# The input panels of block 1 by head halves, with most of them and of the first output panel beside the attention units

## The chip, the cores and the metric

The kernel runs on one core of a Trainium2 chip. Its time is the device time of one launch in microseconds (us), and lower is better. TensorE (PE) does the matrix products, VectorE (DVE), ScalarE (ACT) and GpSimd (POOL) the rest, and SyncE (SP) issues the DMAs.

## What is computed

Two transformer blocks in fp32 on 512 tokens of width 1024. Block 1 is where the change lies:

```python
h = rms_norm(x, norm1_g[l])
proj = h @ w_in[l]                       # 1024 -> q, k, v (512 each: 8 heads of 64) and u (512)
q = rms_norm(q, q_norm_g[l]); k = rms_norm(k, k_norm_g[l])
a = neighbourhood_attention(q, k, v, rpb[l])   # 8 rows x 64 columns, 16 columns wide, with a bias table
p = multiscale_pool(u, w_pool[l], pool_scale[l])
x = x + jnp.concatenate([a, p], axis=-1) @ w_out[l]
x = x + (silu(h2 @ w_gate[l]) * (h2 @ w_up[l])) @ w_down[l]    # h2 = rms_norm(x, norm2_g[l]), 2816 wide
```

Block 2 has a sliding-window attention, a convolution branch, gates and a second feed-forward part, and ends in a norm.

## The kernel before

Activations stand transposed on chip: a chunk is 128 channels by 512 tokens. All weights pass in **panels** of 256 columns, in two blocks of 128 (m = 0, 1), through two slots. For each block SP loads 512 KB into `w_stage`, ACT rounds it to `w_hi` (`high_part`, L539), POOL subtracts the rest into `w_lo` (`low_part`, L462), and PE makes three products of 128x128 by 128x512 for each of 8 chunks k (`step`, L1163): high by high, high by low, low by high. So a panel is 48 products. `open_block` (L1175) waits for the low part and for the bank's last result to have been taken. The order of each engine's work is written out by hand, with semaphores between them.

Block 1 starts so. PE turns x (L1205 to 1212), DVE copies it to `xT` (L814) and makes `h_lo` (L795), ACT makes `h_hi` (L572). Input panels 0 to 7 hold q (0, 1), k (2, 3), v (4, 5) and u (6, 7), and are taken in this order. The norm of x is applied behind the products: ACT squares 8 chunks (L578), DVE adds them (L790, `add_squares`), PE sums over partitions (`norm_sum`, L1197), ACT takes the root (`norm_root`), DVE the reciprocal `rs` (`norm_factor`, L803). Each q and k chunk c is then squared (ACT), summed by head (PE, `qk_sum`, L1214), rooted (ACT, `qk_roots`, L590) and scaled by a reciprocal (DVE, `qk_norm`, L839). v is turned (`turn_v`) and copied (`v_copy`).

Attention has 16 **units**, each two blocks of 128 queries of one head, and goes in pairs on PE (loop at L1328): `score_pair` (L1281, 8 products), `value_pair` of four units back (L1293, 16 products), `turn_probs` of two units back (L1273). DVE reads the scores (L880), ACT makes the exponentials (`exps`, L611), DVE divides (`normalise`, L863). Units 0 to 7 use heads 0 to 3, units 8 to 15 heads 4 to 7. The table `BESIDE1` (L296) lays pieces of panels 6 and 7 between the units' products, one piece being one block and two chunks k, 6 products. `POOL_AT`, `SUMS_AT` and `MEANS_AT` set at which unit the work of the pooling branch is done. Behind the units comes the first output panel (`OUT1`, L1362 to 1372).

```python
        steps1 = [s for steps in beside(IN1 + 6, 2, 1) for s in steps]
        for count in (4, 1, 1, 2, 1, 1, 0, 2, 1, 0, 0, 3, 0, 0, 0, 0, 0, 0, 0):
```

SP loads x and panels 0 and 1, then the small vectors (L410 to 417), panels 2 and 3, 32 short-run DMAs of the attention bias (L425 to 429), and then the rest in order.

## Time and profile before

| what | value |
|---|---|
| median of 3 runs | 1248.16 us (1247.87 to 1249.33) |
| the profiled execution | 1247.56 us |
| its span on the core | 1245.8 us |
| PE busy | 1214.3 us (97%) |
| DVE, POOL, ACT busy | 629.5, 553.1, 486.7 us |
| DMA | 115 MB, mean 92 GB/s |

The span runs from the first to the last instruction that the profiler saw, and the execution's own time is 1.76 us longer. The page gives shares of the whole span. What a stage costs is read from stretches of time and from the timeline of one engine, where the words in brackets behind an instruction are the idle time ahead of it and what ended it.

### The profile page before, as it was taken

The numbers are of one execution on the slowest core, as the hardware profiler recorded it, in microseconds if no ns is written. First come the engines' busy times: TensorE is split into PE (matmuls) and PEld (weight loads), VectorE is DVE, ScalarE is ACT, GpSimd is POOL, SyncE is SP. The second block draws the span as 40 slices with busy tenths as digits, with TensorE's granted clock in tenths as the row PEclk, the third lists the DMA queues.
The fourth block names the chain that finished last, engine by engine and source line by source line (L and its number), as shares of the span: only waits on it lengthen the run. The fifth ranks groups of instructions, "written<-read, shape, count | busy, mean of one in ns | idle before, by whom it ended". The sixth has DMA issues, their size and how long they took to land.

```text
span 1245.8 us, 16589 instructions
## 1 busy us (share of the span) xinstructions
PE 1214.3 (97%) x5568; PEld 986.4 (79%) x5568; DVE 629.5 (51%) x854; ACT 486.7 (39%) x715; POOL 553.1 (44%) x311
## 2 busy tenths in 40 slices
PE   7899899999999999999999999999999999999997
PEld 5677678888888888888877887788888888888876
DVE  6589855432134413466387422266677136622654
ACT  5234634533222222244465432344455234322344
POOL 4393123444444344455423545654355444443441
PEclk9899999999999999999999999999999999999999
DMA  6732113332433333234320223434233333333211
GB/s 189 148 90 87 35 36 100 101 88 80 119 97 90 100 102 93 72 89 118 102 68 27 78 82 101 118 102 118 77 92 105 100 100 88 98 102 102 84 51 68
DMA packets 219505, 115.14 MB, mean 92 GB/s; under 512 B 4195, under 2 KB 217921, under 8 KB 219457
## 3 DMA queue, kind: packets, MB, share of 16 engines
q1 hardware_dynamic: 219441, 114.50, 31.9%
q8 instruction: 30, 0.49, 0.2%
q14 instruction: 18, 0.15, 0.0%
q10 hardware_dynamic: 16, 0.00, 0.0%
HBM read 112.39 MB, written 2.10 MB: 92 GB/s over the span
## 4 chain that ended last, share of the span: by engine, by line
issue 43%; PE 28%; POOL 20%; DVE 4%; ACT 2%; DMA 1%; POOLq 1%; SPq 0%; DVEq 0%; ACTq 0%
PE ps L1170 27%; POOL w_lo L466 19%; DVE sq_sum L790 1%; ACT w_hi L546 1%; DVE mid L1016 1%; DMA w_stage<-in_w_in 1%; DVE mid L783 1%; POOL mid L459 1%; DVE mid L1026 1%; ACT mid L681 0%; DVE h_lo L795 0%; ACT g_hi L686 0%; SPq L373 0%; ACT mid L678 0%; DVE rs L805 0%
## 5 line engine op out<-in xcount | busy, mean ns | idle before, releaser
L466 POOL TENSOR_TENSOR w_lo<-w_stage,w_hi 128x1024 fp32r<-128x1024 f32 x218 | 535.0, 2464 | 666.3 <-ACT w_hi L546 666.2
L1170 PE MATMUL ps<-h_hi,w_hi 128*128 128x512 f32 x1104 | 438.5, 397 | 1.8 <-POOL w_lo L466 1.1
L1170 PE MATMUL ps<-h_hi,w_lo 128*128 128x512 f32 x1104 | 431.3, 391 | 0.0
L1170 PE MATMUL ps<-h_lo,w_hi 128*128 128x512 f32 x1104 | 430.9, 390 | 0.0
L546 ACT ACTIVATE w_hi<-w_stage 128x1024 fp32r<-128x1024 f32 x218 | 227.0, 1056 | 367.9 <-PE ps L1170 364.1
L1170 PEld LDWEIGHTS ps<-h_hi,w_hi 128*128 128x128 f32 x1104 | 208.1, 188 | 51.2 <-issue 7.3
L1170 PEld LDWEIGHTS ps<-h_lo,w_hi 128*128 128x128 f32 x1104 | 208.2, 189 | 44.4 <-issue 2.2
L1170 PEld LDWEIGHTS ps<-h_hi,w_lo 128*128 128x128 f32 x1104 | 207.9, 188 | 44.0
L1170 PE MATMUL ps<-g_hi,w_hi 128*128 128x512 f32 x544 | 212.0, 390 | 2.0 <-DVE g_lo L1028 1.9
L1170 PE MATMUL ps<-g_lo,w_hi 128*128 128x512 f32 x544 | 211.7, 389 | 0.0
L1170 PE MATMUL ps<-g_hi,w_lo 128*128 128x512 f32 x544 | 211.6, 389 | 0.0
L783 DVE TENSOR_TENSOR mid<-ps,rs 128x512 f32<-128x512 f32 x130 | 88.1, 687 | 233.6 <-PE ps L1170 233.5
L979 DVE TENSOR_TENSOR xT<-xT,ps 128x512 f32 x64 | 43.4, 686 | 165.4 <-PE ps L1170 165.3
L1170 PEld LDWEIGHTS ps<-g_hi,w_hi 128*128 128x128 f32 x544 | 102.1, 188 | 24.2 <-DVE g_lo L1028 2.8
L1170 PEld LDWEIGHTS ps<-g_hi,w_lo 128*128 128x128 f32 x544 | 102.1, 188 | 21.3
L1170 PEld LDWEIGHTS ps<-g_lo,w_hi 128*128 128x128 f32 x544 | 102.1, 188 | 21.1
L1016 DVE SCALAR_TENSOR_TENSOR mid<-mid,vec 128x512 f32<-128x512 f32 x88 | 101.7, 1213 | 25.2 <-ACT mid L678 25.2
L1026 DVE TENSOR_TENSOR mid<-mid 128x512 f32<-128x512 f32 x44 | 62.3, 1416 | 27.8 <-ACT mid L684 25.1
L686 ACT ACTIVATE g_hi<-mid 128x512 f32 x44 | 27.8, 632 | 74.7 <-DVE mid L1026 74.7
L684 ACT ACTIVATE mid<-mid 128x512 f32<-128x512 f32 x44 | 27.5, 625 | 72.3 <-DVE mid L1016 72.3
L790 DVE TENSOR_TENSOR sq_sum<-sq_sum,sq 128x512 f32<-128x512 f32 x32 | 47.1, 1473 | 13.7 <-ACT sq L658 13.7
L1028 DVE TENSOR_TENSOR g_lo<-mid,g_hi 128x512 f32 x44 | 31.6, 718 | 43.9 <-ACT g_hi L686 43.9
(141 smaller groups left out, 686.2 us busy)
## 6 DMA issues: line engine op xcount, KB each, us to landing
w_stage<-in_w_up SPq DMA_DIRECT2D x66, 512.0 KB, 3.8
w_stage<-in_w_in SPq DMA_DIRECT2D x50, 512.0 KB, 3.9
w_stage<-in_w_down SPq DMA_DIRECT2D x32, 512.0 KB, 3.6
...
```

What stands on the lines that cost most here:

```text
L459: return pool.affine_select(out=ap, in_=in_, compare_op=cmp, fill=fill, base=base, pattern=pattern, channel_multiplier=mult)
L466: pool.tensor_tensor(w_lo[:, s, c], w_stage[:, s, c], low_of(w_hi[:, s, c]), ALU.subtract).then_inc(w_lo_ready, 1)
L546: act.activation(w_hi[:, s, c], w_stage[:, s, c], ACT.Copy).then_inc(w_hi_ready, 1)
L684: act.activation(gate, gate, ACT.Silu).then_inc(f_silu, 1)
L686: act.activation(chunk(g_hi, 2 * i + j), up, ACT.Copy).then_inc(f_hi, 1)
L783: dve.tensor_tensor(out, bank(par, m), rs[:, :], ALU.mult).then_inc(evacuated, 1)
L790: dve.tensor_tensor(sq_sum[:, :], sq_sum[:, :], squares, ALU.add).then_inc(sq_added, 1)
L979: dve.tensor_tensor(chunk(xT, m), chunk(xT, m), bank(par, e), ALU.add).then_inc(evacuated, 1)
L1016: dve.scalar_tensor_tensor(o, f_in[:, 2 * e + j, 1 - tap:1 - tap + T], col(f"fconv{1 - tap}", c + FC * e), o, ALU.mult, ALU.add)\
L1026: dve.tensor_tensor(up, gate, up, ALU.mult).then_inc(f_prod, 1)
L1028: dve.tensor_tensor(chunk(g_lo, 2 * i + j), up, low_of(chunk(g_hi, 2 * i + j)), ALU.subtract).then_inc(f_ready, 1)
L1170: ins = pe.matmul(bank(par if banks is None else banks, m), a, b, start=first and i == 0, stop=last and i == 2)
```

## The change

The order of the input panels becomes 0, 2, 4, 1, 3, 5, 6, 7: q, k and v of heads 0 to 3 first. The first four panels of the new order and three pieces of the fifth (`AHEAD1`) are done ahead of the units, and the 29 pieces that are left lie beside units 0 to 11. The second half of q, k and v is normed, taken and turned between units, with the roots at units 1 and 4. Of the first output panel, 6 of its 8 chunks lie beside units 12 to 17, and 2 behind the units. At the start, panel 0 is loaded and split in halves of 4 chunks k, its first products stand ahead of the second half of the turns of x, `h_lo` is made from the PSUM bank and not from `xT`, and the squares of x come from the untransposed x with the sum of each token in one accumulator (4 of 128x1024), which DVE spreads on a diagonal for PE's sum. The bias rows come in 16 DMAs, not 32, and ahead of the small vectors. What is computed is the same.

```diff
-        steps1 = [s for steps in beside(IN1 + 6, 2, 1) for s in steps]
...
+        IN1_ORDER = (0, 2, 4, 1, 3, 5, 6, 7)
+
+        QK = [("q", 0), ("q", 1), ("k", 0), ("k", 1), ("q", 2), ("q", 3), ("k", 2), ("k", 3)]
+        QK_PANEL = (0, 0, 1, 1, 3, 3, 4, 4)
+        HALF_QK = len(QK) // 2
...
+        def qk_bank(c):
+            return 5 + c % 2 if c < HALF_QK else 2 * (QK_PANEL[c] % 2) + c % 2
+
+        steps1 = [s for steps in beside(IN1 + 4, 4, 1) for s in steps]
+        AHEAD1, steps1 = steps1[:3], steps1[3:]
...
+        for count in (3, 3, 3, 3, 3, 2, 2, 2, 2, 2, 2, 2, 0, 0, 0, 0, 0, 0, 0):
             BESIDE1.append(steps1[:count])
             steps1 = steps1[count:]
-
-        SUMS_AT = {0: (0, (0,)), 4: (1, (0,)), 5: (1, (1,)), 8: (2, (0,)), 9: (2, (1,)), 10: (2, (2,)),
+        assert not steps1
+
+        def v_bank(a):
+            return ps[:, 6 + a, :] if a < 2 else bank(5, a - 2)
+
+
+        QK_SUMS_AT = {0: (4, 5), 3: (6, 7)}
+        QK_ROOTS_AT = {1: (4, 5), 4: (6, 7)}
+        QK_NORM_AT = {1: 4, 2: 5, 4: 6, 5: 7}
+        K_TAKE_AT, K_SQUARES_AT, V_TAKE_AT, V_TURN_AT = 2, 3, 5, 6
+        SUMS_AT = {7: (0, (0,)), 8: (1, (0, 1)), 10: (2, (0,)), 11: (2, (1, 2)),
                    12: (3, (0,)), 13: (3, (1,)), 14: (3, (2,)), 15: (3, (3,))}
...
+            def load_first(k0, signals):
+
+                for m in range(2):
+                    sp.dma_start(
...
             load_x(0)
-            for n in range(2):
-                load(IN1 + n, n % 2, [cols(w_in[0], n * 256), cols(w_in[0], n * 256 + P)])
...
+            load_first(0, first_landed)
+            load_x(1)
+            load_first(KC // 2, w_landed[0])
+            load(IN1 + 1, 1, [cols(w_in[0], IN1_ORDER[1] * 256), cols(w_in[0], IN1_ORDER[1] * 256 + P)])
...
+            sp.wait_ge(bias_cleared, 1)
+            for c, j, count in BIAS_ROWS:
...
             for tile, r, src in vec_loads[1:]:
                 sp.dma_start(vec_rows[r:r + src.shape[0], tile, :], src).then_inc(vec_landed, 16)
...
-            for n in range(2, 4):
-                load(IN1 + n, n % 2, [cols(w_in[0], n * 256), cols(w_in[0], n * 256 + P)])
...
-            sp.wait_ge(bias_cleared, 1)
...
-            for c in range(16):
-                for dst, shift, first in ((bias_in, c, 7), (bias_in_edge, 0, 15 - c)):
...
-            load_pairs(IN1 + 4, 4, w_in[0], 1024)
+            for n in range(2, 8):
+                load(IN1 + n, n % 2, [cols(w_in[0], IN1_ORDER[n] * 256), cols(w_in[0], IN1_ORDER[n] * 256 + P)])
+                if n == 3:
+                    sp.dma_start(w_pool_sb[:, :, :], w_pool[0].rearrange("g c d -> c g d")).then_inc(pool_w_landed, 16)
...
+            for half, (signal, done) in enumerate(((first_hi, first_lo), (w_hi_ready, w_lo_ready))):
+                for m in range(2):
+                    pool.wait_ge(signal, m + 1)
+                    c = slice(m * HALF + half * FIRST, m * HALF + (half + 1) * FIRST)
+                    pool.tensor_tensor(w_lo[:, 0, c], w_stage[:, 0, c], low_of(w_hi[:, 0, c]),
+                                       ALU.subtract).then_inc(done, 1)
...
+            low_part(1, 1)
+            low_part(2, 0)
+            pool.wait_ge(bias_landed, 16 * len(BIAS_ROWS))
+            pool.wait_ge(sq_added, NT)
+            for h in range(HEADS // 2):
+                bias_tables(h)
+            low_part(3, 1)
+            for h in range(HEADS // 2, HEADS):
+                bias_tables(h)
+            low_part(4, 0)
...
+            def first_high(half, m, signal, done):
+                act.wait_ge(signal[m], 16)
+                c = slice(m * HALF + half * FIRST, m * HALF + (half + 1) * FIRST)
+                act.activation(w_hi[:, 0, c], w_stage[:, 0, c], ACT.Copy).then_inc(done, 1)
...
                 if m < 2:
-                    high_part(0, 0, m)
+                    first_high(0, m, first_landed, first_hi)
+                if m in (4, 5):
+                    first_high(1, m - 4, w_landed[0], w_hi_ready)
             high_part(1, 1, 0)
             high_part(1, 1, 1)
-            for m in range(KC):
-                act.activation(chunk(sq_start, m), chunk(xT, m), ACT.Square).then_inc(x_squared, 1)
...
+            for t in range(NT):
+                for e in range(2):
+                    act.wait_ge(x_landed[e][t], 16)
+                act.activation(sq_start[:, t, :], x_in[:, t, :], ACT.Square,
+                               accum_out=x_sq[:, t:t + 1]).then_inc(x_squared, 1)
...
+                for c in QK_ROOTS_AT.get(u, ()):
+                    qk_roots(c)
+                if u == K_SQUARES_AT:
+                    for c in (6, 7):
+                        qk_squares(c)
...
-            for m in range(KC):
-                add_squares(0, m, chunk(sq_start, m))
+
+            def x_low_of_bank(m):
+                dve.wait_ge(x_scaled, m + 1)
+                dve.scalar_tensor_tensor(chunk(h_lo, m), ps[:, m % 4, :], col("norm1", m),
+                                         low_of(chunk(h_hi, m)), ALU.mult, ALU.subtract)\
+                   .then_inc(h_ready, 1)
...
+            for t in range(NT):
+                dve.wait_ge(x_squared, t + 1)
+                dve.tensor_scalar(sq_sum[:, t * P:(t + 1) * P], ident[:, :], x_sq[:, t:t + 1], None,
+                                  ALU.mult).then_inc(sq_added, 1)
...
-            qk_take(0)
-            for n in range(1, 4):
-                qk_take(n)
-                qk_norm(n - 1)
-            dve.wait_ge(bias_ready, 1)
-            v_take(4)
-            qk_norm(3)
-            v_copy(0)
-            v_copy(1)
-            v_take(5)
+            for c in (0, 1):
+                q_take(c)
+            for c in (2, 3):
+                k_take(c)
+            for c in (0, 1):
+                qk_norm(c)
+            v_take(2)
+            for c in (2, 3):
+                qk_norm(c)
+            for a in (0, 1):
+                v_copy(a)
+            for c in (4, 5):
+                q_take(c)
+            dve.wait_ge(bias_ready, HEADS)
...
+                if u in QK_NORM_AT:
+                    qk_norm(QK_NORM_AT[u])
+                if u == K_TAKE_AT:
+                    for c in (6, 7):
+                        k_take(c)
+                if u == V_TAKE_AT:
+                    dve.wait_ge(qk_ready, len(QK))
+                    dve.memset(sq_sum[:, :], 0.0).then_inc(sum_cleared, 1)
+                    v_take(5)
...
             for m in range(2):
-                open_block(0, m)
+                pe.wait_ge(first_lo, m + 1)
                 for k in range(KC // 2):
                     pe.wait_ge(h_ready, k + 1)
                     step(0, (m,), k, H, k == 0, False, banks=-1)
+                if m == 0:
+                    for c in range(KC // 2, KC):
+                        turn_x(c)
+            for m in range(2):
+                open_block(0, m)
             for k in range(KC // 2, KC):
                 pe.wait_ge(h_ready, k + 1)
...
+
+                        if n in (5, 6):
+                            pe.wait_ge(qk_rooted, HALF_QK + 2 * (n - 5) + m + 1)
+                        if n == 7:
+                            pe.wait_ge(v_ready, 3 + m)
                         open_block(n, m)
                     for kk in (k, k + 1):
                         step(n % 2, [m], kk, H, kk == 0, kk == KC - 1)
...
+            def out1_beside(u):
+                if u in OUT1_AT:
+                    k = OUT1_AT[u]
+                    if k < 4:
+                        pe.wait_ge(heads_ready, k + 1)
+                    else:
+                        pe.wait_ge(pool_ready, k - 3)
+                    if u == min(OUT1_AT):
+                        pe.wait_ge(pool_ready, 2)
+                        for m in range(2):
+                            open_block(OUT1, m)
+                    step(0, (0, 1), k, G, u == min(OUT1_AT), False)
...
+            beside_unit(AHEAD1)
+            pe.wait_ge(qk_ready, HALF_QK)
+            pe.wait_ge(pool_w_landed, 16)
             for u in range(0, SPAN + 1, 2):
-                if u == 0:
...
                         pe.wait_ge(scores_read, u)
+                    if u == UNITS // 2:
+                        pe.wait_ge(qk_ready, len(QK))
                     score_pair(u, unit1, lambda r, h, b: q1[r, h // 2, b * P:(b + 1) * P], keys_of1)
...
-            pe.wait_ge(pool_ready, 3)
-            for m in range(2):
-                open_block(OUT1, m)
-            for a, k in enumerate([4, 5, 6, 0, 1, 2, 7, 3]):
-                if k == 0:
-                    pe.wait_ge(heads_ready, 3)
-                if k == 7:
-                    pe.wait_ge(pool_ready, 4)
-                if k == 3:
-                    pe.wait_ge(heads_ready, 4)
-                step(0, (0, 1), k, G, a == 0, a == KC - 1)
+            pe.wait_ge(pool_ready, 4)
+            step(0, (0, 1), 7, G, False, False)
+            pe.wait_ge(heads_ready, 4)
+            step(0, (0, 1), 3, G, False, True)
```

The instructions in their order show three of these places.

DVE at the norm of x, before; `mid` holds the squared chunks:

```order
L814 COPY xT<-ps 128x512
L795 SCALAR_TENSOR_TENSOR h_lo<-xT,vec,h_hi 128x512 x2
L790 TENSOR_TENSOR sq_sum<-sq_sum,mid 128x512 x8
L821 COPY vec<-ps 128x216
L822 TENSOR_SCALAR neg_sink<-sink 128x8
L805 RECIPROCAL rs<-rms 128x512
```

and now, where `x_sq` holds the sums of each token:

```order
L883 COPY xT<-ps 128x512
L887 SCALAR_TENSOR_TENSOR h_lo<-ps,vec,h_hi 128x512 x2
L899 TENSOR_SCALAR sq_sum<-ident,x_sq 128x128 x4
L902 COPY vec<-ps 128x216
L903 TENSOR_SCALAR neg_sink<-sink 128x8
L873 RECIPROCAL rs<-rms 128x512
```

Eight additions of 128x512 have become four small products with the identity, and `h_lo` reads `ps`.

ACT from the last root of q and k to unit 2, before; L616 are the exponentials:

```order
L596 ACTIVATE mid<-ps,eps 128x512 x2
L546 ACTIVATE w_hi<-w_stage 128x1024 x2
L616 ACT_TABLE_LOAD
L616 ACTIVATE mid,exp_sum<-mid,neg_max 128x256 x2
L546 ACTIVATE w_hi<-w_stage 128x1024
L616 ACTIVATE mid,exp_sum<-mid,neg_max 128x256 x2
L616 ACTIVATE sq,exp_sum<-sq,neg_max 128x256 x2
L623 ACTIVATE mid<-ps 128x512
```

and now (L679 the exponentials, L655 the roots, L646 the squares, L598 the high parts):

```order
L646 ACTIVATE mid<-mid 128x512 x2
L679 ACT_TABLE_LOAD
L679 ACTIVATE mid,exp_sum<-mid,neg_max 128x256 x2
L598 ACTIVATE w_hi<-w_stage 128x1024
L679 ACTIVATE mid,exp_sum<-mid,neg_max 128x256 x2
L655 ACT_TABLE_LOAD
L655 ACTIVATE rms<-ps,eps 128x512
L655 ACTIVATE sq_sum<-ps,eps 128x512
L598 ACTIVATE w_hi<-w_stage 128x1024
L679 ACT_TABLE_LOAD
L679 ACTIVATE sq,exp_sum<-sq,neg_max 128x256 x2
L686 ACTIVATE mid<-ps 128x512
```

Two roots, with a table load on each side, stand between the exponentials of units 1 and 2. Two more stand at unit 4 in the same way.

SP behind the loads of panel 1, before:

```order
L411 DMA vec_rows<-in_conv_w 12x128
L411 DMA vec_rows<-in_ffn_conv_w 44x128 x3
L414 DMA vec_rows<-in_q_norm_g 1x64 x2
L414 DMA vec_rows<-in_k_norm_g 1x64 x2
L416 DMA sink<-in_sinks 128x8
L383 DMA w_stage<-in_w_in 128x8x128 x4
L427 DMA mid<-in_rpb 8x8x233 x32
L430 DMA w_pool_sb<-in_w_pool 128x4x128
```

and now:

```order
L423 DMA w_stage<-in_w_in 128x8x128 x2
L464 DMA mid<-in_rpb 8x8x241 x8
L464 DMA mid<-in_rpb 8x8x240 x8
L468 DMA vec_rows<-in_norm_g 8x128
L468 DMA vec_rows<-in_mix_norm 8x128
L468 DMA vec_rows<-in_ffn_norm 8x128
L468 DMA vec_rows<-in_final_norm 8x128
L468 DMA vec_rows<-in_b_in 34x128
```

The bias rows (`mid<-in_rpb`), half as many, moved from behind panel 3 to ahead of the small vectors (`vec_rows`, `sink`). The loads of panels 2 and 3 come behind the last small vector, as before.

## Rows read from the trace of the kernel before

**Rows 1.** The page: busy time, PE's clock by slice, the two costliest groups that split weights.

```profile
PE 1214.3 (97%) x5568; PEld 986.4 (79%) x5568; DVE 629.5 (51%) x854; ACT 486.7 (39%) x715; POOL 553.1 (44%) x311
...
PEclk9899999999999999999999999999999999999999
...
L466 POOL TENSOR_TENSOR w_lo<-w_stage,w_hi 128x1024 fp32r<-128x1024 f32 x218 | 535.0, 2464 | 666.3 <-ACT w_hi L546 666.2
...
L546 ACT ACTIVATE w_hi<-w_stage 128x1024 fp32r<-128x1024 f32 x218 | 227.0, 1056 | 367.9 <-PE ps L1170 364.1
```

**Rows 2.** Stretches: start:end, busy us (instructions) by engine, PEclk, DMA share, GB/s.

```profile
39.33:48.65 9.32, 9.32 (x27) 6.76 (x27) 6.75 (x10) 1.90 (x4) 0.00 (x0) 0.67 0.65 110
48.65:105.67 57.02, 57.02 (x242) 44.21 (x240) 41.49 (x29) 19.50 (x26) 38.41 (x89) 1.00 0.47 115
105.67:164.81 59.14, 50.52 (x346) 36.47 (x345) 49.28 (x158) 33.20 (x93) 9.88 (x4) 0.94 0.15 44
164.81:175.70 10.89, 10.89 (x50) 9.02 (x49) 1.65 (x4) 1.59 (x4) 0.00 (x0) 1.00 0.01 2
175.70:1245.80 1070.10, 1059.00 (x4804) 868.98 (x4802) 503.39 (x632) 412.20 (x566) 484.51 (x198) 1.00 0.31 92
```

**Rows 3.** Timeline of PE, 12 to 45 us: start, duration, line, instruction, [idle before].

```profile
12.80 3.04 PE L1211 MATMUL ps<-ident,mid 128*128 128x128 f32 x13 [0.28 <-DMA mid<-in_x]
15.49 0.78 PE L1170 MATMUL ps<-h_hi,w_hi 128*128 128x512 f32 x1
...
28.95 0.39 PE L1170 MATMUL ps<-h_hi,w_hi 128*128 128x512 f32 x1
...
39.33 2.07 PE L1199 MATMUL ps<-sq_sum,ones 128*128 128x512 f32 x2 [4.43 <-DVE sq_sum L790]
...
41.63 0.63 PE L1170 MATMUL ps<-h_lo,w_hi 128*128 128x512 f32 x1
```

**Rows 4.** Timeline of DVE, 11 to 46 us.

```profile
11.68 2.34 DVE L795 SCALAR_TENSOR_TENSOR h_lo<-xT,vec,h_hi 128x512 fp32r<-128x512 f32 x1 [0.98 <-ACT h_hi L572]
...
19.16 0.73 DVE L795 SCALAR_TENSOR_TENSOR h_lo<-xT,vec,h_hi 128x512 fp32r<-128x512 f32 x1
...
26.23 13.05 DVE L790 TENSOR_TENSOR sq_sum<-sq_sum,mid 128x512 f32<-128x512 f32 x8 [1.67 <-ACT mid L578]
...
42.16 3.35 DVE L805 RECIPROCAL rs<-rms 128x512 f32<-128x512 f32 x1 [2.52 <-ACT rms L564]
```

**Rows 5.** Timeline of PE in the units, 105 to 165 us.

```profile
111.07 1.13 PE L1288 MATMUL ps<-mid 64*128 64x256 f32 x8 [1.85 <-DVE neg_max L885]
...
151.33 2.08 PE L1288 MATMUL ps<-mid 64*128 64x256 f32 x8 [1.37 <-DVE neg_max L885]
153.34 1.71 PE L1304 MATMUL ps<-mid 128*64 128x128 f32 x16
...
158.56 1.98 PE L1304 MATMUL ps<-mid 128*64 128x128 f32 x16 [1.51 <-ACT mid L623]
...
163.78 1.09 PE L1304 MATMUL ps<-mid 128*64 128x128 f32 x16
```

**Rows 6.** Timeline of ACT: two table loads and an exponential.

```profile
1.37 1.28 ACT L568 ACT_TABLE_LOAD   x1 [1.37 <-PEq L1476]
2.67 0.20 ACT L568 ACTIVATE eps<-eps 128x1 f32<-128x1 f32 x1
...
107.64 0.51 ACT L616 ACTIVATE mid<-mid,neg_max 128x256 f32<-128x256 f32 x1 [4.89 <-DVE neg_max L885]
```

**Rows 7.** Timeline of DVE, 62 to 82 us: the scaling of q and k.

```profile
62.74 3.35 DVE L842 RECIPROCAL mid<-mid 128x512 f32<-128x512 f32 x1 [12.69 <-ACT mid L596]
...
81.30 2.02 DVE L845 SCALAR_TENSOR_TENSOR mid<-mid,vec 128x512 f32<-128x512 f32 x1
```

**Rows 8.** SP's issue of the bias rows, and a 2 us stretch inside.

```profile
30.47 15.28 SPq L427 DMA_DIRECT2D mid<-in_rpb  x32
...
36.00:38.00 2.00, 0.00 (x0) 0.00 (x0) 1.82 (x3) 0.00 (x0) 0.38 (x1) 1.00 0.57 87
```

More of the change, by code:

```diff
@@ L107, in two_blocks @@
         vec_rows = sb("vec_rows", [P, 3, P])
+        x_sq = sb("x_sq", [P, NT])
         mid = sb("mid", [P, 14400])
@@ L153, in two_blocks, with qk_scratch, qk_root @@
         v_t = u_pad
[L154 removed]
+        sq_start = mid[:, 6144:10240].rearrange("p (t d) -> p t d", t=NT)
         BR = 256
[L157 to L158 removed]
+        BIAS_ROWS = [(c, 0, (ROWS - 1) * CB + 24) if c < 8 else (c, 8, (ROWS - 1) * CB + 23) for c in range(16)]
+        bias_in = mid[:, 10240:10240 + HEADS * BR].rearrange("p (h s) -> p h s", h=HEADS)
+        def qk_scratch(c):
+            return win[:, c % 2, 0:T]
+        def qk_root(c):
+            return (rms, sq_sum)[c % 2][:, :]
         q2 = mid[:, 0:2048].rearrange("p (a t) -> p a t", a=4)
@@ L180, in two_blocks @@
         x_landed = [[sem(f"x_landed{t}{e}") for t in range(NT)] for e in range(2)]
+        first_landed = [sem(f"first_landed{m}") for m in range(2)]
+        first_hi = sem("first_hi")
+        first_lo = sem("first_lo")
         norm1_landed = sem("norm1_landed")
@@ new lines, in qk_squares, with qk_roots @@
+            def qk_squares(c):
+                act.wait_ge(evacuated, 2 * QK_PANEL[c] + c % 2 + 1)
+                if c >= 2:
+                    act.wait_ge(qk_summed, c - 1)
+                act.activation(qk_scratch(c), qk_chunk(c), ACT.Square).then_inc(qk_squared, 1)
+            act.wait_ge(eps_ready, 1)
+            def qk_roots(c):
+                act.wait_ge(qk_summed, c + 1)
+                if c >= 2:
+                    act.wait_ge(qk_ready, c - 1)
+                q = QK[c][0] == "q"
+                act.activation(qk_root(c), ps[:, qk_bank(c), :], ACT.Sqrt, scale=1.0 if q else 1.0 / HD,
+                               bias=eps[:, 2:3] if q else eps[:, 0:1]).then_inc(qk_rooted, 1)
@@ L611, in exps @@
+            for c in (2, 3):
+                qk_roots(c)
+            ahead(3, 1)
+            for c in (4, 5):
+                qk_squares(c)
             def exps(u, p):
@@ L1204, in _, with turn_x @@
             pe.transpose(ps[:, 5, 0:KC], vec_rows[0:KC, 0, :], ident[0:KC, 0:KC]).then_inc(norm1_turned, 1)
-            for m in range(KC):
+            def turn_x(m):
                 if m >= 4:
-                    pe.wait_ge(x_ready, m - 3)
+                    pe.wait_ge(h_ready, m - 3)
                 for t in range(NT):
@@ L1256, in _ @@
             pe.wait_ge(const_step, 4)
-            panel(2, 2, H)
-            qk_sum(0)
-            for n in (3, 4):
-                block(n, 0)
-                qk_sum(n - 2)
-                block(n, 1)
-            pe.wait_ge(vec_ready, 1)
-            qk_sum(3)
-            for m in range(2):
-                open_block(5, m)
-                for k in range(KC):
-                    step(1, [m], k, H, k == 0, k == KC - 1)
-                    if (m, k) == (1, 4):
-                        turn_v(0)
-                        turn_v(1)
+            pe.wait_ge(vec_ready, 1)
+            block(2, 0)
+            for c in (0, 1):
+                qk_sum(c)
+            block(2, 1)
+            for c in (2, 3):
+                qk_sum(c)
+            block(3, 0)
+            open_block(3, 1)
+            for k in range(KC):
+                step(1, [1], k, H, k == 0, k == KC - 1)
+                if k == 4:
+                    turn_v(0)
+                    turn_v(1)
             def turn_probs(u, p):
@@ L1350, in _ @@
                     beside_unit(BESIDE1[u + 1])
+                    for c in QK_SUMS_AT.get(u + 1, ()):
+                        qk_sum(c)
                     pool_matmul(u + 1)
+                    out1_beside(u + 1)
                 if 2 <= u < UNITS + 2:
```

185 lines of the change are left out of this document (81 added, 104 removed).

## The prediction

> **What bounds the kernel now.** I read the page first: PE is busy 97% of the span, and its clock is full in all slices but one near the start [rows 1]. So a gain can only come from the 3% in which PE is idle, or from short falls of the clock that a slice of 31 us doesn't show. The stretches say where that is [rows 2]. From 175.7 us to the end PE is busy 1059.0 of 1070.1 us, and no line there changes. Ahead of it, two places lose time. One is the norm of x: the stretch from 39.33 us has a granted clock of 0.67, between its levels of 2.4 and 1.2 GHz, and PE is idle for 4.43 us ahead of it [rows 3]. The other is the units: 59.14 us with 50.52 busy, so 8.62 idle, and a clock of 0.94. The measure of full speed is the first output panel, where 48 products take 10.89 us, 0.227 each [rows 2]; a piece of 6 is 1.36, a block of 24 is 5.45.
>
> The timelines say why. PE starts its first product at 15.49, and the second panel at 28.95; its turns of x run ahead of that, 13 in 3.04 us [rows 3]. The wait at 39.33 ends with the additions of the squares, 8 in 13.05 us, where one such pass over 512 columns elsewhere takes 0.73; `h_lo` also took 2.34 once, beside POOL's split of a weight block [rows 4]. In the units PE waits for the other engines: the scores of the last pair start 1.37 us late, and from there the clock is half: 2.08 us and not 1.13 for the scores, 1.71 and 1.98 and not 1.09 for values [rows 5].
>
> **The change part by part.** PE does the same products as before, so I keep books of what PE's idle and slow time is now, and what replaces it. All against the profiled execution, 1247.56 us (span 1245.8), which is 0.6 below the median of the three runs.
>
> *Start.* Half panels of 256 KB land about a quarter earlier than whole blocks, ACT and POOL need half of 1056 and 2464 ns for one [rows 1], and no turn of the second half of x is ahead. I put the first product at 11.2 us. Then 12 products at half clock (5.1; one is 0.63 long and not 0.39 there [rows 3], so I put them 0.43 apart, not 0.227), 16 turns while the clock comes up (2.3, less than the row's 0.234 each) and 12 more products (2.7) lead to 21.4. There PE waits until about 21.8 for the second half's low part, which hangs on the fifth turn: a copy, `h_hi`, a high and a low part on DVE, ACT, ACT and POOL. 24 products later it is 27.3. Before it was 28.95 [rows 3]. Gain 1.6. Bounds: 0, if the landing of x keeps PE as now, and 4.3, if all 15.49 less 11.2 were kept.
>
> *Norm.* ACT is done with the high parts of panel 1 near 24.2 us; its four squares of 1024 columns, at 1.1 each (a high part of that size is 1056 ns [rows 1]), end near 29, and DVE's four small products near 30. PE comes to `norm_sum` at 33.2, behind block (1, 0) and the vectors' turns. The idle 4.43 goes, and with it the half clock behind it: `norm_sum` and 24 products would take 6.5 (0.65, 0.63 for the first product behind it, 23 of 0.227) and not 9.32 us, so 2.8 more. Gain 7.2. Lower bound 4.4, should the clock fall anyway. Late next is `rs`: norm sum 34.3, root 35.1, the reciprocal of 3.35 [rows 4] to 38.5, the first q chunk to 39.7, when PE wants the bank at 39.8. I take 0.2 for it.
>
> *Bias rows ahead of the vectors.* SP issued 32 of them in 15.28 us while DMA moved 87 GB/s [rows 8]; a DMA is 64 runs of 240 numbers, 61 KB, so 16 are 0.98 MB, some 11 us from about 17.5 on. The vectors then land near 29 us (PE asks at 32.7), panel 2 near 32 to 33 (PE asks at 40). Cost 0; the cover is 4 us. If it is gone, each us late moves ACT's root and all behind it.
>
> *POOL.* Same splits and tables in another order. Four heads' tables, panel 3, and the other four end near 53 us; DVE asks at 69. Cost 0.
>
> *Ahead of the units.* From 40.0: 96 products (21.8), four head sums and two turns of v (3.4), three pieces (4.1), and some 0.4 of changes between kinds. The first scores start near 70 us, not 105.67. DVE's chain to there (four reciprocals of 3.35 with their scalings [rows 7], v, and q) ends at 67 to 69, so PE does not wait.
>
> *Units.* Now 29 pieces and six chunks of the output panel stand between the products, where 12 pieces stood. A pair takes PE some 9.8 us, where DVE has 7 to 8.5 of work. So the 8.62 us of waits go, and so does the half clock at the end: 0.94 + 0.62 + 0.89 for the rows named [rows 5] and some 0.45 for a turn, 2.9 in all.
>
> What comes instead, in the order of PE's list:
> - unit 3: `qk_sum` of chunk 6 needs a square that ACT makes behind the exponentials of unit 3, and DVE first has a reciprocal and scaling (3.35 + 0.8), two k chunks and two scores. 9.2 us against 8.8 on PE: 0.6. A scaling of 2.02 us in place of 0.8 [rows 7] adds 1.2 at worst.
> - unit 4: the first piece of panel 6 writes the bank that holds chunk 6's head sum, and waits for its root. The root stands on ACT behind the exponentials of unit 4 and a table load. Scores read (0.7), two exponentials (1.0), load (1.28) and root (0.7), with hand-overs 3.9 us; PE has one piece to do, 1.4: **2.5 us**.
> - v at unit 6: 0.3. The last value pair waits for the copy behind the last turn, 0.8, and the last chunk of the output panel for heads 6 and 7, 0.5 (now 0.78 and none).
> - some 9 more changes from one kind of product to another at 0.1: 0.9.
>
> On the table load: one is 1.28 us, and the instruction behind it starts 0.02 after its end [rows 6]. The Trainium skill says more (ScalarE: Activation LUTs, What ACT_TABLE_LOAD costs): a switch is the load of about 1283 ns and a drain of about 1380, and its rule is to finish one table set before the next, which speaks against this change. The row shows the load but no such drain, so the sum stays with 1.28; by the page rival 4 would hold.
>
> **The sum.** Gains 1.6 + 7.2 + 8.6 + 2.9 = 20.3. New costs 0.2 + 0.6 + 2.5 + 0.3 + 1.3 + 0.9 = 5.8. Net 14.5: the profiled execution 1233.1, the median 1233.7 us.
>
> **The rivals.**
> 1. *PE is fed nearly throughout*: the new waits overlap (DVE's slack takes up unit 3, ACT comes early at unit 4), and the start keeps its 4.3. The net is 18 to 21, so 1227 to 1230. For it: DVE is busy 49.3 of 59.1 us in the units before [rows 2], and with four scalings and what goes with them (some 17 us) it has 80 us now. Against: the chain at unit 4 has no slack by its order. Chance 0.2.
> 2. *A new wait lets the clock fall.* The drop at 151.33 came with a wait of 1.37 us [rows 5], so 2.5 us at unit 4 could do it too, and so could small waits that add up when DVE's operations last longer beside POOL's splits (ten blocks fall in the units now, four did [rows 2]). The fall at the norm cost 2.8 us; two such falls, or one and 4 us of lengthened DVE work, make a net of 7 to 11: 1237 to 1241. Against it: the scores at 111.07 waited 1.85 us and stayed at full clock [rows 5]. Chance 0.2.
> 3. *The input queue is late*: the bias rows take longer than 11 us beside the rest, panel 2 lands past 36 us, the root of x goes with it, PE waits 3 to 5 us and its clock falls for 5: net 5 to 8, 1240 to 1243. Chance 0.06.
> 4. *A gap behind each table load.* The root at unit 4 starts 1.4 us later, so the wait there is 3.9 us: 1235.1. The row against it is the one with 0.02 us [rows 6]. Chance 0.05. (It is the skill's drain that would make this gap.)
> 5. *Slower than before.* PE's clock stays at half through the units, since every pair has a wait. The units and the output panel hold 222 products, and 0.2 us on each is 44 us, less what idle time they would fill. If over 75 products more than now ran at half clock beside the 14.5, the gain would be gone; all of them make 1250 to 1275. Against it is again the row at 111.07, and a mean clock of 0.94 in the units now [rows 2]. Chance 0.02.
>
> **How the numbers follow.** The main case has 0.47 and spans 1230.5 to 1237; it is the likeliest, so the forecast is its 1233.7. The range takes in rival 1 down to 1227.5, rival 4, and most of rival 2, up to 1239.5. That leaves out 3, 5 and the edges of 1 and 2, some 0.17. What a measurement of this kernel tells from no change is about 0.2%, 2.5 us. All cases but the fifth are faster by more: faster 0.97, within it 0.01, slower 0.02.
>
> **What would show it.** In the profile after, the first scores should start at 69 to 72 us and the first output panel should end at 160 to 163. PE should have no wait at `norm_sum` and full clock from 17 us on; one wait over 2 us for an ACT root at unit 4; two pairs of extra table loads without a gap behind them; and 1070 us from the end of the first output panel on, as before. The forecast is wrong if the first scores start after 75 us, if the clock falls in the units, or if PE's idle time in them is above 8 us.

## The result and the profile after

The changed kernel takes 1242.07 us (median of 5, 1240.47 to 1242.83), the kernel before beside it 1248.16 (5 runs). The ratio is 0.9946, with a 95% interval of 0.9935 to 0.9958: faster, by 6.1 us and not by 14.5. Run again twice, below, it gained 8.4 and 8.6 us (ratio 0.9926 both times). The time lies outside the predicted range, above it. The profiled execution is the one of 1240.47 us, with a span of 1238.7.

The page after, against [rows 1]:

```profile
PE 1210.6 (98%) x5568; PEld 982.2 (79%) x5568; DVE 620.4 (50%) x849; ACT 492.3 (40%) x721; POOL 548.6 (44%) x312
...
PEclk9998999999999999999999999999999999999999
```

The clock is full from the first slice on. The slice below the others is now the fourth (93 to 124 us), where it was the second. Stretches of the changed kernel, cut at the first product, the first wait behind `norm_sum` (for a bank that DVE empties), the first scores, the wait at unit 3, the end of that at unit 4, and the end of the first output panel (start:end, busy us by engine, PEclk, DMA share, GB/s; against [rows 2]):

```profile
11.22:37.71 26.49, 25.82 (x117) 20.13 (x117) 15.38 (x21) 15.88 (x23) 16.50 (x21) 1.00 0.89 223
37.71:68.70 30.99, 30.48 (x132) 23.66 (x131) 25.52 (x21) 9.94 (x13) 23.86 (x72) 1.00 0.32 88
68.70:89.90 21.20, 21.20 (x97) 15.88 (x96) 16.30 (x25) 13.11 (x23) 7.24 (x4) 1.00 0.26 75
89.90:104.13 14.23, 7.77 (x23) 4.15 (x23) 4.55 (x18) 5.84 (x14) 0.00 (x0) 0.76 0.12 37
104.13:167.10 62.97, 60.09 (x384) 44.88 (x385) 52.09 (x134) 31.08 (x78) 11.95 (x5) 1.00 0.14 43
167.10:1238.70 1071.60, 1060.56 (x4804) 870.16 (x4802) 503.06 (x632) 412.31 (x566) 484.55 (x198) 1.00 0.31 91
```

From the first product to the first scores PE is idle for 1.2 us and the clock is full. In the units one stretch stands out: 14.23 us with 7.77 busy and a clock of 0.76. Behind it PE is idle for 2.9 of 63 us. The output panel ends at 167.10 where it ended at 175.70, so 8.6 us were won there; 1.5 of them are gone at the end (1071.60 against 1070.10, all of it in PE's busy time).

PE's timeline of the units (start, duration, line, instruction, [idle before]; against [rows 5]):

```profile
68.70 1.14 PE L1380 MATMUL ps<-mid 64*128 64x256 f32 x8
...
93.96 3.78 PE L1310 MATMUL ps<-mid,head_ones 128*128 128x512 f32 x4 [4.06 <-ACT mid L646]
104.13 0.50 PE L1259 MATMUL ps<-h_hi,w_hi 128*128 128x512 f32 x1 [2.40 <-ACT rms L655]
```

The first wait is that of unit 3, `qk_sum` of chunk 6; the prediction gave it 0.6 us. The second is the root at unit 4, which it gave 2.5. The head sums themselves take 3.78 us for four: that is half clock. DVE and POOL say who made chunk 6 late. First DVE:

```profile
80.18 2.59 DVE L922 SCALAR_TENSOR_TENSOR mid<-mid,vec,rms 128x512 f32<-128x512 f32 x1
...
83.57 0.62 DVE L953 TENSOR_SCALAR mid<-mid,inv_sum 128x256 f32<-128x256 f32 x2
...
87.48 2.90 DVE L922 SCALAR_TENSOR_TENSOR mid<-mid,vec,sq_sum 128x512 f32<-128x512 f32 x1
90.30 1.27 DVE L851 TENSOR_TENSOR mid<-ps,rs 128x512 f32<-128x512 f32 x2
91.50 0.41 DVE L961 CUSTOM_DVE_ANT_0 sq<-ps,mid 128x256 f32<-128x256 f32 x1
...
107.50 0.75 DVE L922 SCALAR_TENSOR_TENSOR mid<-mid,vec,rms 128x512 f32<-128x512 f32 x1
```

and POOL in the same time:

```profile
79.85 2.37 POOL L513 TENSOR_TENSOR w_lo<-w_stage,w_hi 128x1024 fp32r<-128x1024 f32 x1 [3.64 <-ACT w_hi L598]
87.44 2.39 POOL L513 TENSOR_TENSOR w_lo<-w_stage,w_hi 128x1024 fp32r<-128x1024 f32 x1 [5.23 <-ACT w_hi L598]
```

Both scalings ahead of the squares ran into a split of weights (the second block of panel 6, the first of panel 7) and took 2.59 and 2.90 us, where the one at 107.50, with no split beside it, took 0.75. PE stood idle from 89.90 while DVE was in the second. The Trainium skill has this as a rule (SBUF — State Buffer, SBUF: two separate sides): VectorE with two SBUF operands and GpSimd take a port pair in turns, and the later one is fully blocked. The rows agree: 0.75 us of work behind the 2.04 and 2.35 us that are left of the splits would be 2.79 and 3.10, and both scalings are 0.2 shorter than that.

### The profile page after: what moved, and what is told of

The parts are those of the page before. It is cut to its first block, busy times and chain, and to the rows that moved or that the text cites. A ratio compares the mean times of both kernels' runs of the same rounds, so it can differ in the third digit from the quotient of the medians.

```text
span 1238.7 us, 16594 instructions
## 1 busy us (share of the span) xinstructions
PE 1210.6 (98%) x5568; PEld 982.2 (79%) x5568; DVE 620.4 (50%) x849; ACT 492.3 (40%) x721; POOL 548.6 (44%) x312
## 4 chain that ended last, share of the span: by engine, by line
issue 41%; PE 35%; POOL 19%; DVE 1%; DMA 1%; ACT 1%; POOLq 0%; SPq 0%; DVEq 0%; ACTq 0%
PE ps L1259 35%; POOL w_lo L513 19%; DMA w_stage<-in_w_in 0%; DMA mid<-in_x 0%; PE ps L1310 0%; DVE rs L873 0%; ACT w_hi L598 0%; POOLq L574 0%; POOLq L511 0%; DVE xT L883 0%; DVE mid L1246 0%; ACT h_hi L629 0%; DVE h_lo L887 0%; POOL w_lo L532 0%; SPq L415 0%
## 5 line engine op out<-in xcount | busy, mean ns | idle before, releaser
L513 POOL TENSOR_TENSOR w_lo<-w_stage,w_hi 128x1024 fp32r<-128x1024 f32 x216 | 528.0, 2453 | 653.3 <-ACT w_hi L598 653.3
L598 ACT ACTIVATE w_hi<-w_stage 128x1024 fp32r<-128x1024 f32 x216 | 225.5, 1056 | 373.1 <-PE ps L1259 369.4
```

The lines of the kernel that those rows point to most:

```text
L513: pool.tensor_tensor(w_lo[:, s, c], w_stage[:, s, c], low_of(w_hi[:, s, c]), ALU.subtract).then_inc(w_lo_ready, 1)
L598: act.activation(w_hi[:, s, c], w_stage[:, s, c], ACT.Copy).then_inc(w_hi_ready, 1)
```

## The experiments

Two theories for the wait at chunk 6. **L, the lock**: the scalings are slow beside POOL, and that makes the wait. **O, the order**: the takes and squares of k stand behind a reciprocal, a scaling, scores and exponentials, and would be late in any case. Two more stood beside them: **D**, DVE and ACT are held by roots and table loads, and **F**, the clock would fall anyway. All experiments start from the changed kernel. The first runs with POOL kept off, k early, the roots early and the output chunks behind the units had no changed kernel beside them, and the start of an execution varies by 2 us. So I also compare what runs from the first scores to the end of the span: 1238.7 - 68.70 = 1170.0 us in the changed kernel (1170.3 and 1168.8 in two later profiles of it).

### POOL kept off the scalings

`low_part` gets a third argument, the blocks that it splits. Panels 6 and 7 stand ahead of the loop, so the splits of panel 7 are held too:

```diff
+            pool.wait_ge(qk_ready, 5)
+            low_part(6, 0, (0,))
+            pool.wait_ge(qk_ready, 6)
+            low_part(6, 0, (1,))
+            low_part(7, 1)
-            with pool.Fori(3, PANELS // 2) as i:
+            with pool.Fori(4, PANELS // 2) as i:
```

> Edit: the split of panel 6 into its low part on POOL waits, block by block, until chunks 4 and 5 of q are scaled; nothing else moves. Theory L (the two scalings took 2.59 and 2.90 us instead of 0.75 because POOL's splits read the same memory beside them): both scalings come back to about 0.75, the squares of chunk 6 end some 3 us earlier, PE's wait of 4.06 us at the sum of chunk 6 falls to about 1.0, the clock stays full behind it, and the kernel takes 5.5 to 6.5 us less than the changed one. Theory O (the place of the takes and squares behind reciprocal, scaling, scores and exponentials makes the wait, whatever the scalings take): the wait stays over 3 us and the time moves by less than 1 us. Theory D (DVE and ACT are held by the roots and their table loads in units 1 to 3): as O.

Measured: 1236.05 us (4 runs), the kernel before 1249.62 on this chip, ratio 0.989 (0.987 to 0.991). DVE, PE and POOL of this kernel:

```profile
80.53 0.75 DVE L927 SCALAR_TENSOR_TENSOR mid<-mid,vec,rms 128x512 f32<-128x512 f32 x1
...
82.32 1.85 DVE L958 TENSOR_SCALAR mid<-mid,inv_sum 128x256 f32<-128x256 f32 x2
...
87.47 0.75 DVE L927 SCALAR_TENSOR_TENSOR mid<-mid,vec,sq_sum 128x512 f32<-128x512 f32 x1
```

```profile
91.81 1.98 PE L1315 MATMUL ps<-mid,head_ones 128*128 128x512 f32 x4 [1.55 <-ACT mid L651]
99.28 0.51 PE L1264 MATMUL ps<-h_hi,w_hi 128*128 128x512 f32 x1 [2.40 <-ACT rms L660]
```

```profile
81.36 2.40 POOL L513 TENSOR_TENSOR w_lo<-w_stage,w_hi 128x1024 fp32r<-128x1024 f32 x1 [12.17 <-DVE mid L927]
```

The scalings are back to 0.75 us, the wait falls from 4.06 to 1.55, and four head sums take 1.98 and not 3.78 us: the clock stays full. From the first scores on it is 1233.8 - 69.06 = 1164.7 us, 5.3 less: 2.5 of wait, 2.7 of clock (the 22 products between the two waits take 5.07 us here and 7.77 there). L holds for most of the wait and all of the fall behind it. The 1.55 that stays is not all O's. The split that was held now starts at 81.36, and the two passes that normalise probabilities, which stand between the two scalings, take 1.85 us beside it and not 0.62. Without those 1.2 us I estimate that the order alone would leave 0.3.

### k taken early

The two takes of k move ahead of chunk 5's norm in unit 2, and `K_SQUARES_AT` goes from 3 to 2. POOL is as in the changed kernel.

```diff
-        K_TAKE_AT, K_SQUARES_AT, V_TAKE_AT, V_TURN_AT = 2, 3, 5, 6
+        K_TAKE_AT, K_SQUARES_AT, V_TAKE_AT, V_TURN_AT = 2, 2, 5, 6
...
-                if u in QK_NORM_AT:
-                    qk_norm(QK_NORM_AT[u])
                 if u == K_TAKE_AT:
                     for c in (6, 7):
                         k_take(c)
+                if u in QK_NORM_AT:
+                    qk_norm(QK_NORM_AT[u])
```

> Edit: chunks 6 and 7 of k are taken ahead of the norm of chunk 5 in unit 2, and their squares stand behind the exponentials of unit 2 instead of unit 3; POOL is as in the changed kernel. Theories L and O both: no wait at the sum of chunk 6, clock full, 7 us less than the changed kernel (4.06 of the wait, some 3.4 of the half clock, less what a later row of scores gives back); L adds that the scaling of chunk 5 still takes over 2.5 us and costs nothing. Theory F (the clock would have fallen anyway, the wait being only a part of its cause): 4 us less and a granted clock of 0.7 to 0.8 somewhere between 90 and 105 us. Theory D: less than 2 us.

Measured: 1235.76 us (4 runs), ratio 0.9885 (0.9865 to 0.9905). DVE:

```profile
80.66 2.60 DVE L922 SCALAR_TENSOR_TENSOR mid<-mid,vec,rms 128x512 f32<-128x512 f32 x1
...
84.59 1.28 DVE L851 TENSOR_TENSOR mid<-ps,rs 128x512 f32<-128x512 f32 x2
...
89.17 1.82 DVE L922 SCALAR_TENSOR_TENSOR mid<-mid,vec,sq_sum 128x512 f32<-128x512 f32 x1
```

PE:

```profile
90.23 1.88 PE L1310 MATMUL ps<-mid,head_ones 128*128 128x512 f32 x4
...
97.60 0.51 PE L1259 MATMUL ps<-h_hi,w_hi 128*128 128x512 f32 x1 [2.39 <-ACT rms L655]
99.10 0.63 PE L1259 MATMUL ps<-h_hi,w_hi 128*128 128x512 f32 x1
```

The scalings are still slow, and the wait is gone: the lock costs nothing where nothing urgent stands behind it. From the first scores on it is 1164.6 us, 5.4 less and not 7: now the clock falls behind the wait of 2.39 us, where products take 0.63 from 99.10 on. With POOL kept off, the same wait of 2.40 left it full. D is out, since the roots and loads are untouched. F, with its 4 us and its clock of 0.7 to 0.8, is half right: the clock fell at the next wait instead, more briefly (0.89 from 90 to 105 us).

### The roots early as well

```diff
-        QK_ROOTS_AT = {1: (4, 5), 4: (6, 7)}
+        QK_ROOTS_AT = {1: (4, 5), 3: (6, 7)}
```

> Edit: as the kernel with k taken early, and the roots of chunks 6 and 7 stand behind the exponentials of unit 3 instead of unit 4. If the wait of 2.40 us at the root of chunk 6 is the price of its table load standing behind the exponentials of unit 4: that wait goes, PE is fed from 70 to 140 us, and the kernel takes 2 to 2.5 us less than the one with k taken early, 9 to 10 less than the changed one. If the load merely moves (the exponentials of unit 4 now wait for the table): a wait of 1 to 2.5 us appears at the turning of the probabilities of unit 4, and the gain over the kernel with k early is under 1 us.

Measured: 1231.87 us (5 runs), ratio 0.985 (0.9832 to 0.9869). PE waits for nothing between the first scores (70.44) and 134.74:

```profile
90.00:105.00 15.00, 15.00 (x87) 10.90 (x85) 13.59 (x26) 10.03 (x21) 4.06 (x2) 1.00 0.12 35
```

From the first scores on it is 1158.7 us, 5.9 less than with k early and 11.3 less than the changed kernel. That is more than the 2.4 of the wait. The fall behind it (six products 0.43 us apart and not 0.23, and the value pair behind them 1.41 us long and not 1.09, so 1.5) went too. So did one of 1.7 us near the end, of which more below; whether this edit took that one away or it happened not to come is not shown. 0.3 stays without an owner. The load of the table was the price only in its place: it does not come back at the next exponentials.

The same kernel beside the changed one on one chip:

> The changed kernel again, as the measure for the other three of this call: 5 to 8 us less than the kernel before.

> The kernel with k taken early and the roots early once more, beside the changed kernel on one chip: 9 to 11 us less than that, which is the two waits (4.06 and 2.40), the half clock behind the first (3.4) and, where it falls well, that of the last panels (1.5).

Measured: 1240.80 us (6 runs, ratio 0.9926, 0.9908 to 0.9945) and 1230.56 (5 runs, 0.9847, 0.9828 to 0.9865), the kernel before 1249.4. So 10.2 us less than the changed kernel, and 1.5% less than the kernel before. It is the fastest version of this study.

### Both cures together

> Edit: the kernel with k and the roots early, and POOL's two splits of panel 6 kept behind the scalings as in the first experiment. If the slow scalings cost only through the order that the other kernel has mended: the scalings come down from 2.60 and 1.82 us to 0.75 and the time is that of the kernel with the roots early, within 0.5 us. If they still hold up something (the scores of unit 2, the roots): 1 us or more less.

Measured: 1233.80 us (5 runs, ratio 0.987, 0.9851 to 0.9889), on the same chip as the last two: 3.2 us more than without the waits on POOL, where I expected the same or less. DVE and POOL of this kernel:

```profile
91.45 4.17 DVE L958 TENSOR_SCALAR sq<-sq,inv_sum 128x256 f32<-128x256 f32 x2
...
105.80 2.63 DVE L927 SCALAR_TENSOR_TENSOR mid<-mid,vec,sq_sum 128x512 f32<-128x512 f32 x1
```

```profile
90.73 4.74 POOL L513 TENSOR_TENSOR w_lo<-w_stage,w_hi 128x1024 fp32r<-128x1024 f32 x2 [5.74 <-DVE mid L927]
...
105.48 2.39 POOL L513 TENSOR_TENSOR w_lo<-w_stage,w_hi 128x1024 fp32r<-128x1024 f32 x1 [0.75 <-ACT w_hi L603]
```

PE of this kernel:

```profile
109.68 1.25 PE L1323 MATMUL ps<-ident,mid 128*128 128x128 f32 x8 [1.83 <-DVE mid L936]
```

The splits that were held meet two passes that normalise probabilities, which take 4.17 us and not 0.61, and leave DVE 0.8 us late. The last split shown has its old place, 35.18 us behind the first scores in both kernels. But chunk 7's scaling now starts 0.3 us behind the start of that split. With the roots early alone it started at 105.14 us, 0.5 ahead of the split, and took 0.75. Behind it stands the take of v, for which PE waits 1.83 us. The lock was moved, not removed. Most of the rest is the fall of the clock in the last panels (0.93 from 1180 to 1205 us here, 1.00 there).

### The terms of the start, undone one by one

> The changed kernel itself once more, beside the others of this call: 5 to 7 us less than the kernel before, with the wait of 4 us at the sum of chunk 6. Whether the clock falls behind the wait of 1.90 us in the last panels varies from profile to profile and is worth 1.5 us.

> Edit: in the changed kernel the squares of the first norm are taken as before: eight squares of the turned chunks on ACT, eight additions on DVE, one after the other. The prediction's term for this part is 7.2 us (4.4 of idle PE and 2.8 of half clock). If that holds: PE waits 4 us or more at the sum of the norm, the clock falls behind it, and the kernel takes 6 to 8 us more than the changed one. If the clock was the start's and not this wait's: 4 to 5 us more, clock full behind the wait. If the wait is taken up again at the first scores, which stand behind the bias tables: under 2 us.

> Edit: in the changed kernel the first panel's two blocks are loaded, copied and split whole, with the second half of x between them, as before; all else stays. The prediction's term for this part is 1.6 us. Theory A (the term was right): 1 to 2 us more than the changed kernel. Theory B (the earlier and denser start also lets the clock rise some 3 us sooner): 3 to 4 us more, with products of 0.63 us until about 15 us.

On one chip (the kernel before 1249.87): the changed kernel 1241.43 us (6 runs, ratio 0.9926, 0.9907 to 0.9945); the norm undone 1247.75 (12 runs, 0.9965, 0.9946 to 0.9984); the start undone 1243.86 (6 runs, 0.9947, 0.9929 to 0.9965).

Norm undone, PE and its stretch:

```profile
37.16 2.07 PE L1284 MATMUL ps<-sq_sum,ones 128*128 128x512 f32 x2 [4.17 <-DVE sq_sum L855]
```

```profile
37.16:47.00 9.84, 9.84 (x29) 7.20 (x30) 6.74 (x9) 1.89 (x3) 7.45 (x21) 0.69 0.25 68
```

The wait and the fall of [rows 3] are back, and the term is 6.3 us where 7.2 stood. Its 12 runs fall into two groups: nine between 1245.64 and 1249.32, three at 1238.59, 1240.37 and 1241.99, no slower than the changed kernel. The mean granted clock of the three is 0.994 to 0.997, that of the nine 0.991 or 0.992, so what they spare is at least in part slow clock; where, no profile shows.

Start undone, PE:

```profile
13.73 0.79 PE L1254 MATMUL ps<-h_hi,w_hi 128*128 128x512 f32 x1 [3.51 <-POOL w_lo L515]
```

The first product is 1.9 us later than in the changed kernel on this chip (11.83), the first scores 3.2 us later (74.09 against 70.89), and the time 2.4 us. The term was 1.6; the experiment undoes the halves of the first panel only. It lies between the two theories: products take 0.63 us until 20 us here and until 16.7 in the changed kernel on this chip, so more of the start runs at half clock, as theory B has it.

### The output chunks behind the units

`OUT1_AT` is empty and the loop over eight chunks stands behind the units, as before the change.

> Edit: in the changed kernel the six chunks of output panel 0 stand behind the units again, in the order of the kernel before. If they fill waits that the last units have anyway (1.37, 1.51 and 0.78 us at the last scores, turns and values of the kernel before): 3 to 4.5 us more than the changed kernel, with waits of over 1 us between 140 and 165 us. If they only moved work: within 1 us of the changed kernel.

> The changed kernel with the six chunks of output panel 0 behind the units, beside the changed kernel on one chip. By the first look (waits of the last units 7.0 us against 2.9, and a clock of 0.89 between 140 and 170 us): 4 us from the waits and 2 to 3 from the clock, together 6 to 7 us more than the changed kernel.

Measured: 1248.39 us (13 runs, ratio 0.9988, 0.9976 to 1.0001), and on the chip where the changed kernel takes 1240.80, 1247.64 us (12 runs, 0.9986, 0.9975 to 0.9998): 6.8 us for six chunks, where the first expectation was 3 to 4.5. In the second run's profile:

```profile
146.88 1.86 PE L1435 MATMUL ps<-mid,w_pool_sb 128*128 128x512 f32 x2 [3.02 <-DVE mid L1016]
153.71 0.63 PE L1370 MATMUL ps<-ident,mid 128*128 128x128 f32 x4 [0.95 <-ACT mid L686]
156.35 1.09 PE L1396 MATMUL ps<-mid 128*64 128x128 f32 x16 [2.00 <-ACT mid L686]
158.64 2.08 PE L1435 MATMUL ps<-mid,w_pool_sb 128*128 128x512 f32 x2 [0.15 <-DVE mid L1016]
162.03 1.09 PE L1396 MATMUL ps<-mid 128*64 128x128 f32 x16 [0.78 <-ACT mid L686]
```

```profile
140.00:170.00 30.00, 23.09 (x147) 16.12 (x146) 18.61 (x56) 12.10 (x34) 2.35 (x1) 0.89 0.06 19
```

Waits of 6.9 us stand where the changed kernel has 0.54 + 0.91 + 0.47 + 0.78 + 0.18 = 2.9, and the clock is 0.89. The rest, 2.8 us, I put down to that clock. Without these six chunks the change as a whole is worth at most 0.25%.

### A miss: the last units rearranged

```diff
-                   12: (3, (0,)), 13: (3, (1,)), 14: (3, (2,)), 15: (3, (3,))}
-        MEANS_AT, POOL_AT = {8: 0, 9: 1, 12: 2, 16: 3}, {9: 0, 10: 1, 13: 2, 17: 3}
+                   12: (3, (0,)), 13: (3, (1,)), 14: (3, (2, 3))}
+        MEANS_AT, POOL_AT = {8: 0, 9: 1, 12: 2, 15: 3}, {9: 0, 10: 1, 14: 2, 17: 3}
```

> Edit: as the kernel with k taken early and the roots early, and in the last units pool group 2 is multiplied one unit later, and the sums and means of group 3 stand one unit earlier. The waits of 0.90 and 0.47 us at these two products go: 1.0 to 1.4 us less than the kernel with the roots early. If DVE is only loaded elsewhere: new waits at the turned probabilities of units 13 and 14, and no difference.

Measured: 1234.71 us (5 runs), ratio 0.9875 (0.9856 to 0.9895), where the roots early alone gave 0.985 and 0.9847: no gain, by the ratios 2.5 to 3 parts in a thousand worse. The two waits are gone and two others came, 2.6 us more in all, and the clock falls again in the last panels:

```profile
140.77 1.13 PE L1380 MATMUL ps<-mid 64*128 64x256 f32 x8 [1.13 <-DVE neg_max L961]
...
150.58 0.50 PE L1259 MATMUL ps<-g_hi,w_hi 128*128 128x512 f32 x1 [2.80 <-DVE g_lo L1061]
```

The second is the low part of pool group 2. Its product was moved a unit later, the means of group 3 now stand ahead of it on DVE, and a chunk of the output panel hangs on it. Ahead of the first, DVE has a normalising pass of 2.16 us instead of 0.62 beside a POOL split: the lock again.

## Why the prediction was wrong

**The step that failed** is the line on unit 3 in the list of new waits: "9.2 us against 8.8 on PE: 0.6. A scaling of 2.02 us in place of 0.8 adds 1.2 at worst." The wait was 4.06. The step took the cost of VectorE beside GpSimd too low, in number and in size.
- *How many.* There are two scalings ahead of the squares, not one, and each can meet a split. The first, at 80.18, does not stand in the line's sum at all, and it holds up the scores of unit 2 and all that follows.
- *How much.* "At worst" was taken from one slow row [rows 7], 2.02 us, though [rows 4] have a pass of the same kind at 2.34 beside a split, which the prediction itself names. By [rows 1] a whole split of 2.46 us can stand ahead of 0.75, and 2.90 was seen. The two scalings took 1.84 and 2.15 us more than 0.75, 4.0 together, where the line had 1.2 "at worst" and counted none of it.
- *What the runs show.* Keeping POOL off both scalings takes 2.5 us of the wait away. Of the 1.55 left, 1.2 are the same lock on another pass. The order alone, the 0.6 of the line, I estimate at 0.3: that part was not too low.

**Its consequence** was priced as a rival and had 0.2: a new wait lets the clock fall. It did, behind unit 3 and not behind unit 4 as rival 2 had it, and cost 2.7 us in the changed kernel's profile. With both, the wait is 3.5 us too small and the clock 2.7. Rival 2's own sum was 1237 to 1241, and the median lies just above it. It also named lengthened VectorE work, from ten blocks of splits in the units; eight start there.

**The rest of the miss** is a second fall. Behind the wait of 1.9 us ahead of the last panels the clock is full in the kernel before, and low in the changed one for eight products:

```profile
1198.35 0.59 PE L1259 MATMUL ps<-g_hi,w_hi 128*128 128x512 f32 x1 [1.90 <-DVE g_lo L1117]
1198.73 0.63 PE L1259 MATMUL ps<-g_lo,w_hi 128*128 128x512 f32 x1
```

That is the 1.5 us lost behind the output panel, which no step of the prediction had. The prediction said "1070 us from the end of the first output panel on, as before"; it was 1071.6.

Together with 1.9 of small waits on pooled chunks, and less the 1.3 by which the first scores came early (68.70 and not 70), this makes 3.5 + 2.7 + 1.5 + 1.9 - 1.3 = 8.3 us. The profiled execution missed by 7.4 (1240.47 against 1233.1); the 0.9 over is in part costs that were in the sum and did not come: no wait for v, where 0.3 stood, and 0.18 for the last chunk of the output panel, where 0.5 stood. Whether the changes of kind cost their 0.9 is not shown.

**Term by term**, the rest:
- *Start, 1.6*: low. The halves alone measured 2.4 us. The first product is at 11.22 us as forecast, but 0.50 long: the clock was already up, where the prediction had half clock until about 17 us. That was luck of this execution. Two other profiles of the changed kernel have 0.80 for this product, as forecast, and their first scores are 2 us later (70.89 and 70.92 against 68.70).
- *Norm, 7.2*: right in kind, 6.3 measured; no wait at `norm_sum`.
- *Bias rows and POOL's order, 0*: right in the changed kernel's profiles, but not always. No wait of PE there ends with a landed panel or a bias table; the wait for the bank behind `rs`, priced at 0.2, was 0.51, 1.04 and none in three profiles. The kernel with the output chunks behind the units has the same start, and in its slowest execution (1254.90 us, profiled) the way of rival 3 came. ACT's root of x stood behind a high part whose panel landed late, PE waited 3.26 us for the bank, and the clock was half behind it:

```profile
35.45 1.06 ACT L598 ACTIVATE w_hi<-w_stage 128x1024 fp32r<-128x1024 f32 x1 [0.54 <-DMA w_stage<-in_w_in]
...
37.83 0.69 ACT L616 ACTIVATE rms<-ps,eps 128x512 f32<-128x512 f32 x1
```

```profile
43.17 0.76 PE L1259 MATMUL ps<-h_hi,w_hi 128*128 128x512 f32 x1 [3.26 <-DVE mid L912]
```

- *First scores near 70*: 68.70 to 70.92.
- *Units, 8.6 + 2.9*: the waits and the half clock of [rows 5] went. The prediction did not say how much of this hangs on the six output chunks: 6.8 us of it. Small waits on pooled chunks, 0.54, 0.91 and 0.47, were not foreseen.
- *Root at unit 4, 2.5*: 2.40. Tail 0.8: 0.78.
- *Table load*: right without a drain. Loads at 70.43, 74.77, 79.79, 102.09 and 110.36 us take 1.28 each, and where the next instruction was ready it starts 0.01 to 0.02 us after the end:

```profile
74.77 1.28 ACT L655 ACT_TABLE_LOAD   x1
76.07 0.69 ACT L655 ACTIVATE rms<-ps,eps 128x512 f32<-128x512 f32 x1
```

So rival 4 and the drain of the Trainium skill (ScalarE: Activation LUTs, What ACT_TABLE_LOAD costs) have no place here.

Of the signs that the prediction named, first scores near 70 us, the free `norm_sum` and the wait for the root at unit 4 came. The output panel ended at 167.10 us and not at 160 to 163, and the clock fell in the units, which was one of its signs of being wrong.

Without unit 3 the sum comes near, in part by luck. The kernel with k early removes that wait alone and takes 1235.76 us where the kernel before takes 1249.62 on the same chip: 13.9 less, against 15.1 (14.5 and the 0.6 of unit 3). But small waits on pooled chunks and two falls of the clock, which the sum did not have, stand there against costs that it had too high, and the kernel before itself has medians from 1248.16 to 1249.87 us.

## What to carry to other kernels

Where VectorE operations with two SBUF inputs stand ahead of something urgent, price each of them with a whole GpSimd operation in front, not with the longest one that a trace happens to show; then move the urgent step ahead of them rather than hold back GpSimd, which only moves the meeting to the next such operation. A wait of PE is worth its length plus the half clock that may follow, so a new list of waits wants a chance of a fall for each of them, not for one. And filler work between products that wait for other engines can be worth more than the waits: six chunks took 4.0 us of waits away and gave 6.8.

## What the runs showed of the chip

- The same wait leaves the clock full in one kernel and lets it fall in another. Behind 1.90 us ahead of the last panels it is full in the kernel before, in both profiles with the roots early and with the start undone, and it fell in all three profiles of the changed kernel (0.93 from 1180 to 1205 us in the first) and in every other profile. Behind 2.40 us at unit 4 it fell with k early, and not in the changed kernel or with POOL kept off. Behind 4.06 us the 22 products took 7.77, 8.07 and 6.71 us in the three profiles of the changed kernel, where 5.07 is full speed. The length of a wait alone does not tell. The Trainium skill says as much of the rise (TensorE: Matmul & The Clock Gate, What's actually happening): how many products of one kernel run slow varies from run to run. No run here shows what decides it.
- Near the start the lengths of the products tell more than the column of the granted clock. In the changed kernel's profiled execution of 1242.99 us they take 0.63 us from 12.42 to 16.7 us, and the column says 1.00 for 11.22 to 14.00.
- A pass with one SBUF input can be held too. Two passes that normalise probabilities (`TENSOR_SCALAR`, 128x256) take 0.62 us, and 1.85 to 2.16 beside a split (4.17 beside two); here in the kernel with the last units rearranged:

```profile
135.30 2.16 DVE L953 TENSOR_SCALAR sq<-sq,inv_sum 128x256 f32<-128x256 f32 x2
```

  A reciprocal of 128x512 took 3.33 to 3.35 us in every row read, beside a split or not.
- The spread of one kernel's times goes with the clock: the kernel before ran between 1245.21 and 1253.74 us in 51 runs on three chips. The runs under 1249 us have a mean granted clock of 0.991 to 0.995, those above 1251 us 0.984 to 0.991. Five runs with the roots early on one chip, where PE waits least, lie between 1230.43 and 1230.87 us, all at 0.998.
